# Two transformer blocks with 32 experts: the experts' small matmuls set between the blocks of the first layer, and other numbers of places for the experts

## The reference

```python
logits = hf @ router_w + router_b                 # 512 tokens x 32 experts
top_val, top_idx = lax.top_k(logits, 4)
gate = jax.nn.softmax(top_val, axis=-1)
...
u = hf[toks] @ w1[e] + b1[e]                      # 1024 -> 2 x 1024
g_, lin = u[:, :D_FF], u[:, D_FF:]
g_ = jnp.minimum(g_, 7.0)
lin = jnp.clip(lin, -7.0, 7.0)
y = ((lin + 1.0) * g_ * jax.nn.sigmoid(1.702 * g_)) @ w2[e] + b2[e]
...                                               # y times the token's gate, summed over its 4 experts
```

## Time and profile before

| | |
|---|---|
| median of 3 runs | 2054.01 us |
| profiled execution | 2054.17 us |
| its span | 2052.4 us |
| TensorE busy | 1941.4 us (95%) |
| DVE, ACT, POOL busy | 680.6, 365.7, 195.5 us |
| DMA | 499.29 MB, mean 243 GB/s over the span |
| first layer of the experts, L1426 | 626.0 us busy |
| second layer, L1442 | 336.6 us busy |
| loads of expert weights | 384 of 1,024 KB, 14.0 us from issue to landing |

### The profile page before, as it was taken

One profiled execution on the slowest core, in us unless ns is written; L12 is line 12 of the kernel. 1 busy time (PEld: TensorE's weight loads), 2 busy tenths in 40 slices (PEclk: granted clock), 3 DMA queues, 4 the chain that ended last, 5 costly groups with the idle time before them and its releaser, 6 DMA issues.

```text
span 2052.4 us, 37638 instructions
## 1 busy us (share of the span) xinstructions
PE 1941.4 (95%) x15926; PEld 1052.2 (51%) x15926; DVE 680.6 (33%) x1757; ACT 365.7 (18%) x823; POOL 195.5 (10%) x239
## 2 busy tenths in 40 slices
PE   5999999999799999999999999999999869989989
PEld 4476664764435454444444445453444334755854
DVE  6446757431412121212121312122121244177140
ACT  2214632240201111110000001010101012152110
POOL 1020000000001212121111111121212010000000
PEclk8979999999799999999999999999999989999999
DMA  9721222411278999999999999999999883100001
GB/s 299 220 74 62 64 97 87 164 57 63 96 267 323 392 364 391 362 386 401 390 390 388 387 392 395 399 389 406 389 405 389 352 263 120 62 1 1 1 1 41
DMA packets 145105, 499.29 MB, mean 243 GB/s; under 512 B 20882, under 2 KB 89864, under 8 KB 95784
## 3 DMA queue, kind: packets, MB, share of 16 engines
q1 hardware_dynamic: 122192, 464.81, 58.9%
q0 software_dynamic: 16800, 22.95, 5.3%
q10 hardware_dynamic: 5944, 9.09, 1.3%
HBM read 481.34 MB, written 18.22 MB: 243 GB/s over the span
## 4 chain that ended last, share of the span: by engine, by line
PE 80%; DMA 10%; DVE 5%; SPq 2%; issue 1%; ACT 1%; DVEq 0%; ACTq 0%
PE bank L1426 24%; PE bank L1442 13%; PE bank L395 10%; DMA ring<-in_exp_w_dram 9%; PE bank L403 8%; PE bank L798 5%; PE bank L557 3%; PE bank L579 3%; PE bank L568 2%; SPq L890 1%; PE bank L769 1%; PE bank L1415 1%; PE bank L379 1%; DVE arena L745 1%; DMA ring<-in_ada_w_dram 1%
## 5 line engine op out<-in xcount | busy, mean ns | idle before, releaser
L1426 PE MATMUL bank<-ring,arena 128*32 128x512 f32 x5696 | 626.0, 596 | 19.6 <-DMA ring<-in_exp_w_dram 16.4
L1426 PEld LDWEIGHTS bank<-ring,arena 128*32 128x32 f32 x5696 | 180.2, 110 | 440.3 <-issue 392.4
L1442 PE MATMUL bank<-ring,arena 128*32 128x256 f32 x5696 | 336.6, 398 | 13.8 <-DVE dst_r L1818 10.7
L1442 PEld LDWEIGHTS bank<-ring,arena 128*32 128x32 f32 x5696 | 227.3, 115 | 113.8 <-issue 17.6
L395 PE MATMUL bank<-hT,ring 128*128 128x512 f32 x448 | 211.7, 625 | 13.2 <-DVE hT L775 7.5
L1814 DVE COPY arena<-bank 128x12 f32<-128x12 f32 (+2 forms) x32 | 5.4, 170 | 615.9 <-PE bank L1390 586.6
L1037 POOL DMA_INDIRECT expert_sums<-arena,dst_r x87 | 135.0, 1551 | 367.3 <-ACT arena L1175 343.2
L403 PE MATMUL bank<-ring,hT 128*128 128x256 f32 (+1 forms) x768 | 156.4, 363 | 0.0
L395 PEld LDWEIGHTS bank<-hT,ring 128*128 128x128 f32 x448 | 88.2, 201 | 120.3 <-issue 117.0
L403 PEld LDWEIGHTS bank<-ring,hT 128*128 128x128 f32 x768 | 135.5, 190 | 18.4 <-issue 2.4
L1157 ACT ACTIVATE arena<-bank 128x384 f32<-128x384 f32 (+2 forms) x64 | 26.5, 465 | 631.3 <-PE bank L1407 631.3
(11 more groups left out here) (335 smaller groups left out, 1629.1 us busy)
## 6 DMA issues: line engine op xcount, KB each, us to landing
ring<-in_exp_w_dram SPq DMA_DIRECT2D x384, 1024.0 KB, 14.0
ring<-in_ada_w_dram SPq DMA_DIRECT2D x24, 1024.0 KB, 11.0
ring<-in_w_in_dram SPq DMA_DIRECT2D x23, 1024.0 KB, 9.5
ring<-in_w_out_dram SPq DMA_DIRECT2D x8, 1024.0 KB, 5.0
expert_sums<-arena POOLq DMA_DIRECT2D x5, 512.0 KB, 4.7
arena<-in_x_dram ACTq DMA_DIRECT2D x1, 2048.0 KB, 12.6
ring<-in_w_in_dram SPq DMA_DIRECT2D x8, 256.0 KB, 5.2
h_rows<-arena ACTq DMA_DIRECT2D x4, 512.0 KB, 3.3
```

The source lines that it names most:

```text
L1426: mm = pe.matmul(bank[g][QUAD * c:QUAD * (c + 1), :].rearrange("p (h n) -> p h n", h=2), rowsT[:, k, QUAD * g:QUAD * (g + 1)], w[:, :, SW ...
L1442: mm = pe.matmul(bank[4 + g // 2][QUAD * c:QUAD * (c + 1), SW * (g % 2):SW * (g % 2 + 1)], actT[:, j, g, QUAD * q:QUAD * (q + 1)], w[:, c, :],
```

## The change

Two things are changed.

The list of places has 87 groups instead of 89: two places of four groups where there were four, 19 of three for 17, and 11 of two as before. Place 0 has three groups where it had four, and the sizes are mixed evenly along the list, where all of the four-group places stood at 0, 1, 4 and 7. The last place has two groups as before.

On TensorE the small pieces move between the blocks of the first layer, through a function `between(k)` that is called after block k. The two halves of turn_hidden come after blocks 1 and 2 (in stage 1 after 5 and 6), spread after block 3 with the wait for ACT's copies of the outputs (y_ok) ahead of it, indices after block 4, and the two halves of turn_rows after blocks 5 and 6 (in stage 1 behind the first layer, as before). The b2 matmul stays behind the first layer, now behind a wait for ACT's copies of the turned rows (xt_ok) instead of the turned hidden rows (at_ok); the wait for DVE's use of bank 7 (b2_ok) moves to the next stage, ahead of the second half of turn_hidden. On DVE the addition of the b2 result moves from the start of an iteration to just ahead of its wait for the first layer, behind the first bias, targets, sources and the one-hot rows of a later place.

```diff
--- before.py
+++ after.py
@@ -61,7 +61,7 @@
 def expert_places():
 
 
-    quads = [4] + [4, 2, 3] * 3 + [3, 2, 3] * 7 + [2]
+    quads = [3, 3, 2, 3, 2, 3, 3, 2, 3, 4, 3, 2, 3, 2, 3, 3, 2, 3, 3, 2, 3, 2, 3, 4, 3, 2, 3, 3, 2, 3, 3, 2]
     ranks, n = [0] * NEXP, 1
     for size in (4, 3, 2):
         for at in range(1, NEXP):
@@ -1399,25 +1399,25 @@
                                    stop=True)
                 mm.then_inc(sg.rows, 1)
 
-            def turn_rows(sg, n, quads):
+            def turn_rows(sg, n, quads, halves=range(2)):
                 rows = QUAD * quads
                 pe.wait_ge(sg.got, n)
-                for a in range(2):
+                for a in halves:
                     for k in range(4):
                         mm = pe.transpose(bank[6 + a][:, rows * k:rows * (k + 1)],
                                           xg[0:rows, P * (4 * a + k):P * (4 * a + k + 1)], ident[0:rows, 0:rows])
                     mm.then_inc(sg.xt, 1)
 
-            def turn_hidden(sg, n, quads):
+            def turn_hidden(sg, n, quads, halves=range(2)):
                 pe.wait_ge(sg.act, n)
-                for j in range(2):
+                for j in halves:
                     for g in range(quads):
                         mm = pe.transpose(bank[6 + j][:, P * g:P * (g + 1)], act_t[:, g, :].rearrange("p (n j) -> p j n", j=2)[:, j, :], ident[:, :])
                     mm.then_inc(sg.at, 1)
 
 
 
-            def first_layer(sg, rowsT, quads, wait_slot, used):
+            def first_layer(sg, rowsT, quads, wait_slot, used, between=lambda k: None):
                 for k in range(ND):
                     wait_slot(k)
                     w = ring[:, k, :, :].rearrange("p a b -> p (a b)").rearrange("p (h n) -> p h n", h=2)
@@ -1428,6 +1428,7 @@
                                            start=(k == 0), stop=(k == ND - 1))
                     if used:
                         mm.then_inc(w1_used, 1)
+                    between(k)
                 if not used:
                     mm.then_inc(sg.u, 1)
 
@@ -1478,36 +1479,44 @@
 
                 def wait_slot(s):
                     pe.wait_ge(landed[s], 16 * ((n if s < 8 else n - 1) + FILLS[s]))
+
+                def between(k):
+                    if k == 2 and n - 1 in B2_AT:
+                        pe.wait_ge(b2_ok, n - B2_AT[0])
+                    if n >= 2 and k in (1, 2):
+                        turn_hidden(main, n, QUADS[n - 1], [k - 1])
+                    if n == 1 and k in (5, 6):
+                        turn_hidden(main, n, QUADS[n - 1], [k - 5])
+                    if k == 3:
+                        if n >= 2:
+                            pe.wait_ge(main.y_ok, PARTS_BY[n - 1])
+                        if n + 1 < NEXP:
+                            if n == 0:
+                                pe.wait_ge(main.dst, 1)
+                                pe.wait_ge(main.meta, 2)
+                            spread(main, n + 2, QUADS[n + 1])
+                    if k == 4 and n + 2 < NEXP:
+                        indices(main, n + 3, route[:, :, n + 2, :], QUADS[n + 2])
+                    if k in (5, 6) and n + 1 < NEXP and n != 1:
+                        if n >= 2:
+                            pe.wait_ge(main.at_ok, 2 * n)
+                        turn_rows(main, 16 * (n + 2), QUADS[n + 1], [k - 5])
                 if n < NEXP:
                     pe.wait_ge(main.xt_ok, 2 * (n + 1))
-                if n >= 2:
-                    turn_hidden(main, n, QUADS[n - 1])
-                if n < NEXP:
                     if n >= 1:
                         pe.wait_ge(main.u_in, n)
-                    first_layer(main, xgT[n % 2], QUADS[n], wait_slot, True)
+                    first_layer(main, xgT[n % 2], QUADS[n], wait_slot, True, between)
+                else:
+                    turn_hidden(main, n, QUADS[n - 1])
+                    pe.wait_ge(main.y_ok, PARTS_BY[n - 1])
                 if n == 1:
-                    turn_hidden(main, 1, QUADS[0])
-                if n >= 2:
-                    pe.wait_ge(main.y_ok, PARTS_BY[n - 1])
+                    pe.wait_ge(main.at_ok, 2 * n)
+                    turn_rows(main, 16 * (n + 2), QUADS[n + 1])
                 if n in B2_AT:
                     t = n - B2_AT[0]
-                    pe.wait_ge(main.at_ok, 2 * n)
+                    pe.wait_ge(main.xt_ok, 2 * (n + 2))
                     pe.matmul(bank[7][:, :], b2_keep[:, P * t:P * (t + 1)], gatesT, start=True, stop=True)\
                       .then_inc(b2_t, 1)
-                if n + 1 < NEXP:
-                    if n == 0:
-                        pe.wait_ge(main.dst, 1)
-                        pe.wait_ge(main.meta, 2)
-                    spread(main, n + 2, QUADS[n + 1])
-                if n + 2 < NEXP:
-                    indices(main, n + 3, route[:, :, n + 2, :], QUADS[n + 2])
-                if n + 1 < NEXP:
-                    if n >= 1:
-                        pe.wait_ge(main.at_ok, 2 * n)
-                    if n in B2_AT:
-                        pe.wait_ge(b2_ok, n - B2_AT[0] + 1)
-                    turn_rows(main, 16 * (n + 2), QUADS[n + 1])
                 if n >= 1:
                     if n + 1 < NEXP:
                         pe.wait_ge(main.dst, n + 2)
@@ -1877,11 +1886,6 @@
             dve.wait_ge(b1_in, 64)
             link(dve.transpose(b1T.rearrange("p k e -> p (k e)"), b1_rows))
             for n in range(NEXP):
-                if n in B2_AT:
-                    t = n - B2_AT[0]
-                    dve.wait_ge(b2_t, t + 1)
-                    dve.scalar_tensor_tensor(out=resT[:, t, :], in0=bank[7][:, :], scalar=mod[:, 40 + t:41 + t],
-                                             in1=resT[:, t, :], op0=ALU.mult, op1=ALU.add).then_inc(b2_ok, 1)
                 if n == 0:
                     e = 0
                 else:
@@ -1895,6 +1899,11 @@
                     sources(main, n + 3, QUAD * QUADS[n + 2])
                 if n + 3 < NEXP:
                     who_at(n + 3)
+                if n in B2_AT:
+                    t = n - B2_AT[0]
+                    dve.wait_ge(b2_t, t + 1)
+                    dve.scalar_tensor_tensor(out=resT[:, t, :], in0=bank[7][:, :], scalar=mod[:, 40 + t:41 + t],
+                                             in1=resT[:, t, :], op0=ALU.mult, op1=ALU.add).then_inc(b2_ok, 1)
                 dve.wait_ge(w1_used, 8 * (n + 1))
                 swiglu(main, n + 1, QUADS[n])
             to_last = meta_r[(NEXP - 1) % 4]
```

## The result

The changed kernel takes 2021.81 us (median of 4 runs, 2018.8 to 2022.66) against 2053.27 for the kernel before on the same chips. The ratio is 0.9845, 95% interval 0.9833 to 0.9856: 31.5 us less by the medians, 31.8 by the ratio. The forecast was 2025, 29 less.

What follows compares the result with a forecast made beforehand. Expert stage bound by TensorE first and DMA later, with near-equal bounds after the change (1610 and 1611). 1611 plus 10 still lost gives 1621 against 1650: 29 us less, 2025 us from 2054; range 2010 to 2046.

Steps and rivals of the forecast that it cites:

- The bound and the loss: Expert stage: the weight stream can't be shortened, early dry time is paid at the end; 29 us lost in five slices.
- The DMA bound: Expert stage after the change: 368 weight transfers at 2.79 us plus landing and tail end at 1611 us at best.
- the 10: Dry stream still expected on top of the DMA bound: 3 us under place 0 and 7 around place 9.
- TensorE's sum: Expert stage on TensorE: groups 901, small matmuls 91, breaks 45, b2 matmuls 10, in all 1047 us, ending at 1610.
- the break c: Price of interrupting first-layer blocks for small matmuls: 0.25 us each, six a stage in 30 stages, 45 us.
- Rivals A: Breaks between first-layer blocks cost 0.36 us: TensorE bounds, 15 us less, 2039 us; chance 0.17.
- B: Breaks between first-layer blocks expose the whole drain, 0.54 us or more: 15 us slower, 2069 us; chance 0.07.
- Rival C: Short blocks lower TensorE's clock to 1.2 GHz for 1.7 us a stage, 52 us: slower, 2066 us; chance 0.04.
- The start of the stage: Start of the expert stage on TensorE: left at 555.1 us in the sum.
- The two groups' DMA: Gathers and adds of the two groups dropped from the list: 1.3 us less DMA.
- The waits that were costed at nothing: New waits ahead of first-layer blocks (y_ok, turned hidden rows, turned rows, xt_ok): all hidden, 0 us.

Runs made afterwards that it cites:

- test 1: The kernel before with the new list of 87 groups alone, small matmuls left in their old places: 2021.83 us, ratio 0.9851.
- test 2: The changed kernel with the old list of 89 groups, small matmuls still between the blocks: 2050.42 us, ratio 0.9986.
- test 3: The changed kernel with the same 87 groups in another order, four-group places at 1 and 4: 2035.36 us, ratio 0.9914.
- test 6: The changed kernel with four groups at place 0 again, 88 groups: 2034.51 us, ratio 0.9907.
- test 11: The changed kernel with the same 87 groups, places 1 and 2 of two groups each: 2015.82 us, ratio 0.9823.
- test 4: The changed kernel with half of the second layer left out on TensorE, all weights still loaded: 2018.67 us, ratio 0.9834.
- test 7: The changed kernel with 89 groups evenly spread, fours at places 9, 15, 23 and 29, three at place 0: 2030.86 us, ratio 0.989.
- test 5: The changed kernel with 147 more breaks, full-width two-column matmuls between groups in blocks 5 to 7 of first layers: 2067.53 us, ratio 1.0072.
- test 8: The kernel with half of the second layer left out (2018.7 us), with the experts' indirect adds into DRAM left out too: 1962.85 us, ratio 0.9562.
- test 9: The changed kernel with the last place's second weights loaded into ring slots 0 to 3, released by its own first layer: 2022.17 us, ratio 0.9848.

## Why the prediction was right

The bound and the loss. That each us in which the stream ran dry early is paid at the end held in tests 1, 2, 3, 6 and 11. To see it, add up (1.03 - share)/1.03*25 over the twelve slices from 550 to 850 us and set it beside the length of the stage:

| | groups | lost by 850, us | stage, us |
|---|---|---|---|
| before | 89 | 40.1 | 1095.1 |
| test 2 | 89 | 37.1 | 1092.0 |
| test 3 | 87 | 26.0 | 1077.7 |
| test 6 | 88 | 25.3 | 1078.1 |
| changed | 87 | 15.3 | 1067.7 |
| test 1 | 87 | 14.0 | 1067.1 |
| test 11 | 87 | 8.7 | 1061.0 |
| test 4 | 87 | 15.1 | 1060.8 |
| test 7 | 89 | 17.9 | 1075.6 |
| test 5 | 87 | 19.2 | 1109.7 |

In the first seven rows the stage shrinks with the loss, by 3.1 us for 3.0 in test 2 and by 34.1 for 31.4 in test 11. In the last two it does not: there TensorE bounds. Test 4 loses what the changed kernel loses and is 6.9 us shorter, which is what TensorE still adds to the changed kernel. The DMA bound was put at 1056 us from the stage's start (1611 - 555.1), with nothing lost; test 4 takes 1060.8, with the early loss in it. The changed kernel stands 12 above the bound, and 10 had been allowed. The total came out, its parts did not. 7 of the 10 were to be lost around place 9, and next to nothing was: the share is 1.01 to 1.04 from 850 to 950 us, around its first layer (834 to 866) and its second (902 to 916). TensorE had caught up by then and waited 1.4 us for weights just ahead of it. The loss that was put at 3 under place 0 was about 7, an estimate from the slices from 550 to 625 (9.0 + 3.9 + 1.7, less the 7.6 us before the first issue at 557.6). Most of the rest is the 6.9 us of TensorE that test 4 takes away: in the changed kernel the second layer of place 30 starts at 1598.1, in test 4 at 1593.4. That these errors nearly cancel is luck.

TensorE's sum. I had 1047; test 5 gives 1044. Of it the break c: 0.25 taken, 0.14 shown in the layer, and the halves of a block cost the fixed part again (0.44 for two transposes where four cost 0.68), so 42 us over the other terms (1002), 0.23 a break. Rivals A (0.36) and B (the drain exposed) are out. The 0.84 us of idle weight loads at each break agree with the rule of the Trainium skill (TensorEngine Tiling (Array Packing), Key Properties) that a change of tiling mode drains TensorE. No run here shows that the drain is their cause; the price of a break is 0.14 by the starts.

The clock. Rival C, whose 1.7 us are 12.25 less 10.57, is out: the granted clock is 1.00 in every slice from 600 to 1625 us. The Trainium skill (TensorE: Matmul & The Clock Gate, Part 4) says that a transpose doesn't count as busy in the same way as a matmul; with pieces this short between blocks no fall came of it. That the clock stopped falling was right and worth next to nothing (tests 1 and 2). On what brings the gain the prediction left the question open, and its time is right without an answer: it counted the move of the small matmuls on TensorE's side only, and with both bounds at 1611 and 1610 it did not say which part of the change would bring the gain. The list brings all of it, the rest nothing that can be told beside the new list, and 3 us beside the old one.

Three terms were mis-sized. The start of the stage, which the sum left at 555.1: 3.1 us earlier, which I did not have; 1.7 of it is the router's small matmuls, now 96 columns wide (from 541.2 to 555.1 before, 539.8 to 552.0 after), and the rest varies from one execution to another (places 0 of three groups start between 549.8 and 553.7, and two executions of the changed kernel at 552.0 and 550.7). The two groups' DMA: 1.3 us by bytes, while an add costs 0.66 (test 8), so at least 1.3 for the adds alone and the gathers beside them; in the table the stages with 87 groups are 2 to 3 us shorter than their loss says. And the losses under place 0 and around place 9, as above; test 11 got about 6 us of the first back. The sum also let place 0 run at full speed: the granted clock is 0.50 until about 557.8 us, where 12 records take 2 us and at 1.00 24 do.

The waits that were costed at nothing cost nothing: in the changed kernel no line of TensorE waits for the gate product, the gathers or b2; it waits for weights (11.7 and 6.2 us), once for 2.1 ahead of place 1 and for 1.3 before the last layer.

## What to carry to other kernels

Where a stream of loads and an engine are both nearly full, add up each one's bound, and then look at where the stream runs dry: time lost before a backlog exists is paid in full at the end, and neither a faster engine nor a steadier clock buys it back later. So give the first stages the least work, and spread the heavy ones; the order of the stages was worth 14 to 20 us here (test 3, test 11), two groups less 9, and the finer placing of small work nothing that could be told. Check such a sum part by part afterwards: here the total of the losses was right and their places were not. To learn which of two near bounds holds, leave out much of the engine's work and see that the time stays (test 4), or add work until its waits are gone (test 5).

## What was not expected of the hardware

An indirect add of 128 rows of 1 KB into DRAM costs a full stream 0.66 us, twice the 0.33 of its bytes (test 8). A full-width piece between 32-column blocks costs 0.14 us over its own matmuls, though weight loads ahead of it idle for 0.84 instead of 0.30. Four loads of 1 MB issued some 20 us sooner into a full stream left the landing of those ahead of them where it was, 27.32 us after the issue for 27.30 (test 9).
